# Decays moved forward, differences in PSUM, a reordered short convolution, and splits dealt out in the triangular inverse

## The reference

```python
def token_mix(h, w_in, gdn_conv_w, gdn_a_log, gdn_dt_bias, gdn_norm_w, sc_conv_w, w_out):
    proj = h @ w_in
    sb_qkv, gdn_qkv, gdn_z, gdn_a, gdn_b, sc_bch = jnp.split(proj, [...], axis=-1)
    o_sb = stick_breaking_attention(sb_q, sb_k, sb_v)          # 4 heads of 64
    gdn_qkv = jax.nn.silu(causal_dwconv(gdn_qkv, gdn_conv_w))
    g_q = l2_normalize(g_q) * (GDN_HEAD_DIM ** -0.5)
    g_k = l2_normalize(g_k)
    beta = jax.nn.sigmoid(gdn_b)
    log_decay = -jnp.exp(gdn_a_log) * jax.nn.softplus(gdn_a + gdn_dt_bias)
    o_gdn = gated_delta_rule_chunked(g_q, g_k, g_v, log_decay, beta)   # 4 heads of 128
    o_gdn = gated_rms_norm(o_gdn, gdn_z, gdn_norm_w)
    sc_b, sc_c, sc_h = jnp.split(sc_bch, 3, axis=-1)
    o_sc = sc_b * causal_dwconv(sc_c * sc_h, sc_conv_w)
    return jnp.concatenate([o_sb, o_gdn, o_sc], axis=-1) @ w_out

def gated_delta_rule_chunked(q, k, v, g, beta):
    gcum = jnp.cumsum(g, axis=-1)
    decay = jnp.exp(jnp.where(incl, gcum[..., :, None] - gcum[..., None, :], -jnp.inf))
    m = jnp.where(strict, jnp.einsum('nbhik,nbhjk->nbhij', k_beta, k) * decay, 0.0)
    t_inv = lax.linalg.triangular_solve(eye + m, eye, left_side=True, lower=True)
    u = t_inv @ (v * beta)
    w = t_inv @ (k_beta * jnp.exp(gcum))
    qk = (q @ k.T) * decay
    # then a scan over the chunks that carries a state per head
```

## Time and profile before

| | |
|---|---|
| median of three runs | 3470.26 us |
| the profiled execution, its span | 3469.21 us, 3467.4 us |
| PE busy | 3342.7 us (96%) |
| DVE, ACT, POOL busy | 1408.3, 1365.4, 1476.0 us (41, 39, 43%) |
| mean granted clock of TensorE | 0.987 |
| DMA | 281.70 MB, mean 81 GB/s |

### The profile page before, as it was taken

The page is one execution under the profiler, slowest core; times in us unless marked ns, Lnnn a source line. Parts: engine busy times, 40 slices in busy tenths (PEclk is TensorE's granted clock), DMA queues, the critical chain, the costliest instruction groups (busy, mean ns, idle before and its releaser), DMA issues.

```text
span 3467.4 us, 45465 instructions
## 1 busy us (share of the span) xinstructions
PE 3342.7 (96%) x16418; PEld 2766.5 (80%) x16418; DVE 1408.3 (41%) x2428; ACT 1365.4 (39%) x2184; POOL 1476.0 (43%) x1111
## 2 busy tenths in 40 slices
PE   8999999899999999999988999988999999999998
PEld 7888876788888888887777888877888888887777
DVE  2221455552214622044465322174365266244533
ACT  3222435542224522232554322266355255454543
POOL 5544433055543555434312554435454354353322
PEclk9999999999999999999999999999999999999999
DMA  4222212022222222222201222222221222231111
GB/s 156 97 97 97 86 61 67 1 86 96 97 97 85 88 96 96 97 80 85 67 25 49 95 96 94 97 101 91 79 74 63 74 78 67 76 125 66 55 51 61
DMA packets 76758, 281.70 MB, mean 81 GB/s; under 512 B 8512, under 2 KB 8640, under 8 KB 76224
## 3 DMA queue, kind: packets, MB, share of 16 engines
q1 hardware_dynamic: 75600, 274.66, 23.7%
q10 hardware_dynamic: 1008, 4.98, 0.4%
HBM read 277.51 MB, written 2.10 MB: 81 GB/s over the span
## 4 chain that ended last, share of the span: by engine, by line
PE 88%; DVE 6%; ACT 3%; issue 2%; POOL 0%; DVEq 0%; ACTq 0%; POOLq 0%
PE ps L1869 16%; PE ps L1871 16%; PE ps L1870 16%; PE ps L1941 4%; PE ps L1943 4%; PE ps L1942 4%; PE ps L2398 2%; PE ps L2412 2%; PE ps L1978 2%; PE ps L1980 2%; PE ps L1979 2%; PE ps L2337 1%; PE ps L2339 1%; PE ps L2338 1%; PE ps L2381 1%
## 5 line engine op out<-in xcount | busy, mean ns | idle before, releaser
L565 POOL TENSOR_TENSOR w_lo<-raw,w_hi 128x512 fp32r<-128x512 f32 x1028 | 1379.6, 1365 | 1712.8 <-ACT w_hi L631 1712.8
L1869 PE MATMUL ps<-x_hi,w_hi 128*128 128x512 f32 x2560 | 1022.6, 399 | 1.1 <-DVE b_q L1665 1.0
L1871 PE MATMUL ps<-x_hi,w_lo 128*128 128x512 f32 x2560 | 997.9, 390 | 0.0
L1870 PE MATMUL ps<-x_lo,w_hi 128*128 128x512 f32 x2560 | 997.4, 390 | 0.0
L631 ACT ACTIVATE w_hi<-raw 128x1024 fp32r<-128x1024 f32 x514 | 541.2, 1055 | 1001.4 <-PE ps L1871 522.4
L1869 PEld LDWEIGHTS ps<-x_hi,w_hi 128*128 128x128 f32 x2560 | 481.7, 188 | 109.4 <-issue 9.7
L1870 PEld LDWEIGHTS ps<-x_lo,w_hi 128*128 128x128 f32 x2560 | 481.7, 188 | 105.4 <-issue 8.6
L1871 PEld LDWEIGHTS ps<-x_hi,w_lo 128*128 128x128 f32 x2560 | 481.1, 188 | 101.9
L1274 DVE TENSOR_TENSOR T<-T,ps 128x512 f32<-128x512 f32 x66 | 45.3, 687 | 496.6 <-PE ps L1871 490.2
L585 POOL TENSOR_TENSOR square_parts<-T,square_parts 128x512 fp32r<-128x512 f32 (+1 forms) x71 | 87.5, 1234 | 255.0 <-ACT square_parts L977 255.0
L1978 PE MATMUL ps<-h_hi,w_hi 128*128 128x512 f32 (+1 forms) x440 | 153.2, 348 | 0.0
(11 more groups left out here) (331 smaller groups left out, 5123.8 us busy)
## 6 DMA issues: line engine op xcount, KB each, us to landing
raw<-in_weights SPq DMA_DIRECT2D x514, 512.0 KB, 3.3
Y<-in_x_t SPq DMA_DIRECT2D x1, 2048.0 KB, 8.0
mem<-in_mem_t ACTq DMA_DIRECT2D x2, 1024.0 KB, 7.1
out_t<-Y SPq DMA_DIRECT2D x8, 256.0 KB, 2.2
ple_p<-in_p_t ACTq DMA_DIRECT2D x2, 512.0 KB, 5.5
mat<-in_mats SPq DMA_DIRECT2D x1, 768.0 KB, 11.7
masks<-in_masks ACTq DMA_DIRECT2D x1, 768.0 KB, 9.0
rope<-in_rope_a ACTq DMA_DIRECT2D x1, 512.0 KB, 9.9
```

Of the source, the lines that this page charges most:

```text
L565: ins = pool.tensor_tensor(g.wl[:, k, part], g.raw[:, k, part], g.wh[:, k, part], ALU.subtract)
L1869: mm(out, wh[:, c], xh[:, kc, :], start=kc == 0, stop=False)
L1870: mm(out, wh[:, c], xl[:, kc, :], start=False, stop=False)
L1871: ins = mm(out, wl[:, c], xh[:, kc, :], start=False, stop=kc == DC - 1)
```

## The change

Seven things are changed in the two mixers.

1. The attention's heads start at unit 5 and not 7, the norms at 20 and not 22, the decays at 23 and not 25. The banks are dealt out anew for it, and the attention's values are transposed behind unit 7 into banks 6 and 7.
2. In `decays` the difference stays in PSUM bank 0, the upper clip and the causal mask are one instruction (a minimum with a matrix of 0 and -30000, `M_CAUSAL`), and the product with the mask behind the exponent is gone.
3. Transposes of keys and values, ACT's key copies and DVE's value scaling stand behind units 25 to 28, one chunk each.
4. `join_x` of steps 0 and 1 stands in the middle of unit 28's tile; DVE's `step(0)` and `step(1)` stand before its copy of that tile. `keep_clock` is gone.
5. ACT copies the attention's results out of PSUM at unit 24; their splits, those of the short convolution and the Silu of z are dealt out over steps 7 to 24 of the inverse.
6. The short convolution's weight tiles come as c, h, c, h, gate, gate; DVE reads h and the gates from PSUM instead of copying them first.
7. GpSimd scales the queries of a chunk behind that chunk's decay group, between weight splits. The upper half of weight unit 32 of the mixer is made in the recurrence.

The diff, cut to what follows from these:

```diff
@@ constants
-M_ONES, M_IDENT, M_UPPER, M_SUFFIX, M_DIAG, M_LEVEL = range(6)
+M_ONES, M_IDENT, M_UPPER, M_SUFFIX, M_DIAG, M_CAUSAL, M_LEVEL = range(7)
-SB_START, SB_STEP = 7, 4
-V_QKN, V_DECAY = 22, 25
+SB_START, SB_STEP = 5, 4
+V_VT, V_GATES, V_SBO = 7, 8, 24
+V_QKN, V_DECAY, V_TURN = 20, 23, 25
@@ mix_bank
-    return v % 4 if v < V_CONV else 3 + (v - V_CONV) % 3
+    return v % 4 if v < SB_START else 3 + (v - SB_START) % 3
+def sb_out(g, t):
+    return g.T[:, (6, 0)[t], :]
@@ pool_program
-        pool.wait_ge(s.eg_done, 4 * m + 4)
-        pool.wait_ge(s.kk_mm, 4 * m + 4)
         for n in range(NT):
+            low_many(at, BASE[f"mix{m}"] + V_DECAY + 1 + n + RING + 1)
+            at = BASE[f"mix{m}"] + V_DECAY + 1 + n + RING + 1
+            pool.wait_ge(s.eg_done, 4 * m + n + 1)
+            pool.wait_ge(s.kk_mm, 4 * m + n + 1)
             q = g.CV[:, 0:4, n * P:(n + 1) * P]
@@ act_program, mixer
+            if v == 28:
+                act.preload_act_table(ACT.Silu)
+                act.wait_ge(s.unit_done, u0 + 29)
...
-            hi(u0 + v + 4)
+            if v < 28:
+                hi(u0 + v + 4)
...
+            if v >= V_TURN:
+                n = v - V_TURN
+                for k in range(n, NT) if n == 2 else range(n, min(n, 1) + 1):
+                    weights = g.small[:, 6, 4 * k:4 * k + 4]
+                    act.wait_ge(s.kd_in, 4 * m + k + 1)
+                    link(fn(weights, weights, ACT.Exp))
+                act.wait_ge(s.kt_done, 4 * m + n + 1)
+                for h in range(HEADS):
+                    ins = fn(g.KD[:, n, h * P:(h + 1) * P], ps[:, 6, h * P:(h + 1) * P], ACT.Copy,
+                             scale=g.small[:, 6, 4 * n + h:4 * n + h + 1])
+                ins.then_inc(s.kd_done, 1)
...
+            if v == V_SBO:
+                act.wait_ge(s.sbo_done, 4 * m + 4)
+                act.wait_ge(s.gb_mm, 4 * m + 1)
+                for k in range(2):
+                    fn(sb_out(g, k), ps[:, 6 + k, :], ACT.Copy).then_inc(s.so_done, 1)
...
-            if v in (17, 21):
+            if v in (17, 19):
...
-        for t in range(2):
-            act.wait_ge(s.sbo_done, 4 * m + 2 * t + 2)
-            mix_hi(m, t, t, ps[:, 6 + t, :])
...
-        fn(g.small[:, 6, :], g.small[:, 6, :], ACT.Exp).then_inc(s.kd_out, 1)
...
-            mix_hi(m, 2 + t, 6 + t, g.PR[:, 12 + 3 * t, :])
...
+            if j in (7, 9):
+                act.wait_ge(s.so_done, 2 * m + 2)
+                mix_hi(m, (j - 7) // 2, (j - 7) // 2, sb_out(g, (j - 7) // 2))
+            if j in (11, 13):
+                k = (j - 11) // 2
+                act.wait_ge(s.proj_evac, 29 * m + V_SC + 5 + k)
+                mix_hi(m, 2 + k, 6 + k, g.PR[:, 12 + k, :])
+            if j in (15, 18, 21, 24):
+                k = j // 3 - 5
+                act.wait_ge(s.proj_evac, 29 * m + V_Z + k + 1)
+                fn(g.PR[:, k, :], g.PR[:, k, :], ACT.Silu).then_inc(s.z_done, 1)
...
+                if n == 0:
+                    hi(u0 + 32)
@@ dve_program, mixer
+            if k in (0, 2):
+                v.tensor_copy(c, src).then_inc(s.proj_evac, 1)
+                return
+            v.tensor_tensor(c, c, src, ALU.mult).then_inc(s.proj_evac, 1)
...
+        def gate_short(t, src):
+            v.tensor_tensor(g.PR[:, 12 + t, :], g.PR[:, 12 + 2 * t, :], src, ALU.mult).then_inc(s.proj_evac, 1)
@@ decays
-            t4, t5, t6 = (g.T[:, k, :] for k in (4, 5, 6))
+            t4, t5, diff = g.T[:, 4, :], g.T[:, 5, :], ps[:, 0, :]
...
-            link(v.tensor_tensor(heads(t6), heads(ps[:, 0, :]), over_cols(5, n), ALU.subtract))
-            link(v.tensor_scalar(t4, t6, 0.0, None, ALU.min))
-            v.tensor_scalar(t5, t6, -1.0, 0.0, ALU.mult, ALU.min).then_inc(s.dec_in, 1)
+            dve.wait_ge(s.kd_in, e + 1)
+            link(v.tensor_tensor(heads(diff), heads(diff), over_cols(5, n), ALU.subtract))
+            v.tensor_tensor(heads(t4), heads(diff), over_heads(g.mat[:, M_CAUSAL, :]), ALU.min)
+            v.tensor_scalar(t5, diff, -1.0, 0.0, ALU.mult, ALU.min).then_inc(s.dec_in, 1)
             dve.wait_ge(s.dec_out, e + 1)
-            link(v.tensor_tensor(heads(t4), heads(t4), over_heads(upper), ALU.mult))
@@ step(j), the former body of the loop of joins
+            if j in (8, 10):
+                mix_low(m, j // 2 - 4, j // 2 - 4, sb_out(g, j // 2 - 4))
+            if j in (12, 14):
+                mix_low(m, j // 2 - 4, j // 2, g.PR[:, 6 + j // 2, :])
@@ the loop over the units
+            if w == 28:
+                for j in range(2):
+                    step(j)
...
+            if w >= V_TURN:
+                n = w - V_TURN
+                dve.wait_ge(s.vt_done, 4 * m + n + 1)
+                v.tensor_tensor(g.CV[:, 8:12, n * P:(n + 1) * P], heads(ps[:, 7, :]), over_cols(4, n), ALU.mult)\
+                    .then_inc(s.vb_done, 1)
+            if w == 27:
+                for j in range(2):
+                    coupling(j)
+                for h in range(2):
+                    v.memset(g.XS[64 * h:64 * h + 64, :, :, 64 - 64 * h:P - 64 * h], 0.0).then_inc(s.xzero_done, 1)
+        for j in range(2, STEPS):
+            step(j)
@@ pe_program
-    def keep_clock(count, bank):
...
+            if kc == DC // 2 and joins is not None:
+                pe.wait_ge(s.m_done, 4 * joins + 4)
+                for j in range(2):
+                    join_x(joins, j)
...
+            if v >= V_TURN:
+                n = v - V_TURN
+                cols = slice(n * P, (n + 1) * P)
+                if n:
+                    pe.wait_ge(s.kd_done, 4 * m + n)
+                else:
+                    pe.wait_ge(s.cvs_done, 12 * m + 12)
+                    pe.wait_ge(s.so_done, 2 * m + 2)
+                for h in range(HEADS):
+                    ins = nc.tensor.transpose(ps[:, 6, h * P:(h + 1) * P], g.CV[:, 4 + h, cols], ident)
+                ins.then_inc(s.kt_done, 1)
+                if n:
+                    pe.wait_ge(s.vb_done, 4 * m + n)
+                for h in range(HEADS):
+                    ins = nc.tensor.transpose(ps[:, 7, h * P:(h + 1) * P], g.CV[:, 8 + h, cols], ident)
+                ins.then_inc(s.vt_done, 1)
...
-        for j in range(STEPS + 1):
+        for j in range(2, STEPS + 1):
             if j < STEPS:
-                join_x(j)
+                join_x(m, j)
+            if j == 3:
+                pe.wait_ge(s.kd_done, 4 * m + 4)
+                pe.wait_ge(s.vb_done, 4 * m + 4)
```

More of the change, by code:

```diff
@@ L1858, in weight, with tile @@
         return g.wh[:, u % RING, :], g.wl[:, u % RING, :]
-    def tile(u0, i, out, xh, xl, mid=()):
+    def tile(u0, i, out, xh, xl, mid=(), joins=None):
         wh, wl = weight(u0)
@@ L2012, in stats @@
             .then_inc(s.stat_done, 1)
-    def keep_clock(count, bank):
-        for _ in range(count):
-            mm(ps[:, bank, :], ones, g.mat[:, 0:4, :].rearrange("p a n -> p (a n)"), start=True, stop=True)
     def rms_stats(i, part, first, end):
@@ L2615, in matrices @@
     out[:, M_SUFFIX] = j >= i
+    out[:, M_CAUSAL] = np.where(j <= i, 0.0, NEG)
     out[:, M_DIAG] = np.where(i <= j, NEG, 0.0)
```

202 lines of the change are left out of this document (79 added, 123 removed).

## The result

| | before | after |
|---|---|---|
| median of the runs, us | 3470.52 (3469.72 to 3471.13, 4 runs) | 3438.88 (3438.00 to 3439.96, 4 runs) |
| profiled execution, time / span, us | 3469.21 / 3467.4 | 3438.67 / 3436.9 |
| mean granted clock | 0.987 | 0.992 |

The ratio is 0.991 (95% interval 0.9898 to 0.9922): 31.6 us less by the medians, 30.5 us less by the two spans. The prediction was 3440.

The account below looks back on a forecast made before the run. PE, busy 96% of the span, bounds the kernel. Seams of 51.97 us less 2 x (7.5 + 0.4 + 3.2) = 22.2 gain 29.8 us: 3469.2 becomes 3439.4, median 3440, range 3432 to 3452.

Parts of the forecast that it names:

- X0 and X1: First products of inverse steps 0 and 1, eight transposes in unit 28's tile on PE: 0.9 us plus 0.1.
- wait before X1: PE's wait in unit 28's tile for DVE's mask products, late if GpSimd's splits fall on them: 0.4 us, at worst 1.0.
- waits between decay groups: PE's waits for the decays of the chunk before, about 1.4 us over three pitches, should go.
- tile 28's end to X4: PE from unit 28's last matmul to the first join of level 1, step 4's first product: 2.6 us.
- insertions in the inverse: Four DVE and eight ACT instructions moved into the inverse's loop of joins: 3.2 us per mixer, bounds 0 and 7.5.
- The seam: PE's stretch from unit 28's last matmul to level 1's first join, 25.65 and 26.32 us; 7.5 us forecast in its place.
- The difference in PSUM: The decays' in-place subtraction, taken at 0.68 us; DVE's path 1.0 us shorter, only 0.2 by the PSUM-operand rule.
- By the shares they fit, by the order they don't: Engine busy shares in the join loop leave room for the inserted 7.5 us; instruction order makes them late nearly in full.
- Free insertions: Rival: the join loop's gaps take the inserted instructions and no mask product is late: 3433 us, chance 0.12.
- In full: Rival: inserted instructions cost 7.5 us per mixer and the start inside tile 28 is late: 3450 us, chance 0.19.
- The clock: Rival: PE falls to 1.2 GHz in the 8 us behind unit 28, 4 us per mixer: 3448, chance 0.05.
- The overlap broken: Rival: each of twelve inserted instructions loses a full 2.45 us period of the join loop: 3493 us, chance 0.03.

Follow-up runs that it names:

- The early couplings: Changed kernel with couplings 0 and 1 issued one unit earlier on DVE, behind the column of unit 26: 3436.43 us.
- the run in SBUF: Changed kernel with the difference of the decays written to SBUF instead of back into its PSUM bank: 3443.01 us.
- the run with the splits in the gap: Changed kernel with each of DVE's four splits in the inverse one place up, ahead of the subtraction into delta_e: 3435.57 us.
- the runs with a wait of 3.24 and of 4.37 us: Changed kernel with all four splits and four Silu back ahead of the joins, 3442.57 us; with decays back beside units 25 to 28, 3450.82 us.

## Why the prediction was right, point by point

The terms for the first mixer:

| step | predicted, us | measured, us |
|---|---|---|
| fourth decay group, three pairs of transposes | 2.63 + 2.6 | 2.64 + 3 x 0.87 = 5.25 (a pair is 8.99 - 8.12) |
| X0 and X1 in tile 28 | 1.0 | 1.02 (595.91 to 597.69, less the wait) |
| wait before X1 | 0.4, up to 1.0 | 0.76, second mixer the same |
| waits between decay groups | -1.4 | 26.02 - (25.22 - 0.87) = -1.67 |
| tile 28's end to X4 | 2.6 | 2.60 |
| insertions in the inverse | 3.2, from 0 to 7.5 | 32.96 - 30.35 = 2.61 |
| both mixers | -29.8 | -30.5 (spans) |

The measured terms leave 7.96 + 2.61 = 10.6 us per mixer of seams that had 51.97 together, a gain of 30.8 for the 30.5 of the spans. Forecast were 11.1. The mechanisms came as forecast, but that the time was met within 1.1 us is in part luck: per mixer, 0.6 us too much for the insertions and 0.3 too little gain from the waits between groups stand against 0.4 too little for the wait before X1. (The waits between groups are 26.02 - 24.54 = 1.48 by the forecast's own numbers, not 1.4; the 0.1 us changes nothing.)

1. The seam. That it would shrink to a few microseconds was read off PE's order and DVE's rows, and came out to the tenth. The undone moves show what carries it: 12 us from the decays' move and 5 from the dealt-out transposes. With 3.7 for the splits and Silu and 4.1 for the operands in PSUM they make 24.7; where the 6.9 us left come from was not shown. They may belong to parts that I did not undo alone, to pairs of parts, or to the drift.
2. The start inside tile 28. I had the right mechanism, GpSimd's split beside the couplings, and took too little: two couplings took 3.24 us, 0.76 of it late. The early couplings show that it is just this, and that it costs 0.9 us.
3. The difference in PSUM. I let the row of 1.23 us beside GpSimd decide against the rule on operands in PSUM, and the run in SBUF shows that this was the right way round. My reason was too weak, though: I counted on a shorter instruction at one place, and not on the fact that an operand in PSUM takes the instruction out of GpSimd's way wherever GpSimd runs. The section of the Trainium skill cited above, "Who interferes with whom", states it, and I had not weighed it; it bears on the wait in point 2 as well. With pitches of 8.12 and 8.99 for my 8.2 and 9.1, no wait is left between the groups.
4. The insertions. DVE's four cost 0.60 to 0.61 each, as I said, visible as PE's waits for `delta_ea`; for ACT's eight I charged 0.8, and 2.61 - 4 x 0.61 leaves 0.2 (0.5 at most by the run with the splits in the gap; the 30.35 us of before began at a low clock, so neither is exact). By the products Y it is some 0.15 us, at the Silu alone. This is the term that was mis-sized most. "By the shares they fit, by the order they don't" held, and the gap version shows that the order is a matter of one place: one place up, they fit.
5. The rivals. Free insertions: refuted by PE's four waits. In full: refuted, 2.61 of 7.5. The clock: it stayed at 1.00, with no wait above 0.8 us left between the decays and the inverse's end; the runs with a wait of 3.24 and of 4.37 us there show the clock of 0.50 that this rival spoke of. The overlap broken: 2.61 / 12 = 0.2 us per insertion, where it decides from 1.5.
6. What I named as signs of a wrong forecast did not come: no tile of the units 17 to 24 waited for weights, the loop grew by 2.6 us and the wait of 4.3 us stayed.

## What to carry to other kernels

Price an instruction that is put into a full pipeline by what is queued behind it and how long that could wait, and try it one place earlier before calling the place full. Before moving work between DVE and GpSimd, or choosing where an operand lives, look which instructions run at the same time: where all operands of both lay in SBUF, one of them waited for the other here. Where the granted clock is at half behind a wait of PE and PE's own work follows, the wait costs more than its length (1.6 to 2.4 us more for 4.3), and products of constants in it gave that part back; where PE went on waiting they gave nothing.
